# A two-layer streaming encoder on eight cores: weight loads on ScalarE's DMA queue, paired x transfers in flight together, a fourth x slot, the small first group of layer 2 batched, the first sums on VectorE

## What is computed

```python
xn = rms_norm(x, lp['norm_mix'])
proj = xn @ lp['w_in']                      # q | k | v | pool_in | two gates
q = rms_norm(q, ...); k = rms_norm(k, ...)
a = swa_prompt(q, k, v, lp['sinks'])        # each 64-frame chunk reads itself and two before it
pl = pool_mixer(p_ext, pos, w_pool, pool_scale)   # trailing means over 2/4/8/16, minus the token
mix = (g[:, :, 0] * (a @ lp['w_br_attn']) + g[:, :, 1] * (pl @ lp['w_br_pool'])) @ lp['w_out']
x = x + mix
...
h = xn2 @ w_up                              # 1024 -> 2 * 2816
hc = conv_b + sum(conv_w[j] * h_ext[:, j:j + T] for j in range(3))
y = (gelu(gate) * val) @ w_down
x = x + y
```

## Time and profile before

| | |
|---|---|
| runs (us) | 3847.88, 4010.42, 4087.85; median 4010.42 |
| the profiled execution | 3838.31 us, span 3836.7 us on its slowest core |
| spans of the eight cores | 3823.3 to 3836.7 us |
| mean granted TensorE clock | 0.947 to 0.953 of full speed |
| busy in the span | PE 87%, DVE 56%, ACT 40%, POOL 31% |
| chain that ended last, by engine | PE 62%, DMA 17%, DVE 6%, POOL 5%, ACT 4%, issue 4%, SP's queue 1% |

### The profile page before, as it was taken

How to read it: one execution, slowest core, us unless ns; L and a number is a source line. 1 busy time by engine, 2 the same in 40 slices (tenths; PEclk the granted TensorE clock), 3 DMA queues, 4 the chain that set the end, 5 groups by cost and what they waited for, 6 DMA issues and landing times.

```text
span 3836.7 us, 54933 instructions; the slowest of 8 cores (3823.3 to 3836.7 us)
## 1 busy us (share of the span) xinstructions
PE 3345.6 (87%) x17810; PEld 1621.7 (42%) x17810; DVE 2135.0 (56%) x3383; ACT 1545.1 (40%) x2432; POOL 1186.7 (31%) x1084
## 2 busy tenths in 40 slices
PE   1579999996599999999975879999966999999999
PEld 0344444442244444444432434444423455555554
DVE  1345455542376776666643444555426766666666
ACT  1244444431234555444433434433314444444444
POOL 1234443321123333322234333333213222333322
PEclk9789999998799999999987989999988999999999
DMA  6326666446623333333353223233252222222221
GB/s 128 69 74 132 127 130 128 122 109 165 185 79 103 92 85 90 95 98 101 106 170 92 50 82 97 88 94 104 76 192 91 81 73 80 80 79 79 79 64 40
DMA packets 186666, 384.37 MB, mean 100 GB/s; under 512 B 32880, under 2 KB 112400, under 8 KB 178384
## 3 DMA queue, kind: packets, MB, share of 16 engines
q1 hardware_dynamic: 181088, 324.00, 28.0%
q0 software_dynamic: 5296, 56.86, 9.6%
HBM read 368.09 MB, written 115.41 MB: 126 GB/s over the span
## 4 chain that ended last, share of the span: by engine, by line
PE 62%; DMA 17%; DVE 6%; POOL 5%; ACT 4%; issue 4%; SPq 1%; DVEq 0%; ACTq 0%; POOLq 0%
PE psb L413 61%; DMA xsl_67<-xT 3%; POOL win_114 L419 1%; DMA xsl_67<-xm 1%; POOL win_115 L419 1%; DMA xsl_66<-xT 1%; DMA xst__146<-xT 1%; DMA xsl_67<-x 1%; POOL PT_121 L419 1%; DMA xst__147<-xT 1%; DMA xsl_66<-x 1%; DMA xsl_66<-xm 1%; DMA xsl_68<-x 1%; ACT P_0_118 L416 1%; DVE xn_71 L422 1%
## 5 line engine op out<-in xcount | busy, mean ns | idle before, releaser
L419 POOL TENSOR_TENSOR actT<-ug_94,uv_97 128x480 bf16<-128x480 f32 (+3 forms) x126 | 148.7, 1180 | 1057.1 <-ACT ug_94 L416 939.6
L416 ACT ACTIVATE ug_94<-psb,pv 128x480 f32<-128x480 f32 (+3 forms) x144 | 106.4, 739 | 698.2 <-PE psb L413 520.5
L422 DVE SCALAR_TENSOR_TENSOR ug_94<-psb,pv,ug_94 128x480 f32<-128x480 f32 (+3 forms) x288 | 202.7, 704 | 137.5 <-ACT hso L416 73.5
L422 DVE SCALAR_TENSOR_TENSOR uv_97<-psb,pv,uv_97 128x480 f32<-128x480 f32 (+3 forms) x288 | 202.3, 702 | 17.2 <-issue 0.6
L422 DVE SCALAR_TENSOR_TENSOR ug_96<-psb,pv,ug_96 128x480 f32<-128x480 f32 (+3 forms) x252 | 177.6, 705 | 52.4 <-ACT ug_96 L416 27.9
L422 DVE SCALAR_TENSOR_TENSOR ug_95<-psb,pv,ug_95 128x480 f32<-128x480 f32 (+3 forms) x252 | 177.4, 704 | 22.8 <-ACT ug_95 L416 6.7
L419 POOL TENSOR_TENSOR actT<-ug_95,uv_98 128x480 bf16<-128x480 f32 (+3 forms) x126 | 148.7, 1180 | 128.9 <-ACT ug_95 L416 116.4
L422 DVE SCALAR_TENSOR_TENSOR uv_99<-psb,pv,uv_99 128x480 f32<-128x480 f32 (+3 forms) x252 | 177.0, 702 | 14.7 <-DVE uv_99 L422 0.9
L422 DVE SCALAR_TENSOR_TENSOR uv_98<-psb,pv,uv_98 128x480 f32<-128x480 f32 (+3 forms) x252 | 177.3, 704 | 14.0 <-DVE uv_98 L422 0.5
L419 POOL TENSOR_TENSOR actT<-ug_96,uv_99 128x480 bf16<-128x480 f32 (+3 forms) x108 | 127.4, 1179 | 159.3 <-ACT ug_96 L416 120.8
L413 PE MATMUL psb<-xn_71,w_up_83 128*128 128x482 bf16 (+3 forms) x576 | 122.4, 373 | 55.3 <-DVE xsl_68 L422 55.3
(11 more groups left out here) (317 smaller groups left out, 7352.0 us busy)
## 6 DMA issues: line engine op xcount, KB each, us to landing
wb<-wun POOLq DMA_DIRECT2D x42, 1024.0 KB, 9.9
xsl_68<-x SPq DMA_DIRECT2D x35, 512.0 KB, 4.1
xsl_68<-xT SPq DMA_DIRECT2D x31, 512.0 KB, 5.1
xsl_66<-x SPq DMA_DIRECT2D x31, 512.0 KB, 4.9
xsl_67<-x SPq DMA_DIRECT2D x30, 512.0 KB, 5.0
xsl_66<-xT SPq DMA_DIRECT2D x29, 512.0 KB, 5.9
xsl_67<-xT SPq DMA_DIRECT2D x28, 512.0 KB, 5.3
xm<-xsl_67 SPq DMA_DIRECT2D x27, 512.0 KB, 3.3
```

The costliest lines, as they stand in the source:

```text
L416: S.op("act", lambda e: e.activation(out=out, in_=in_, func=func, **kw), reads=reads, writes=writes)
L419: S.op(eng, lambda e: e.tensor_tensor(out=out, in0=a, in1=b, op=op), reads=reads, writes=writes)
L422: S.op("dve", lambda e: e.scalar_tensor_tensor(out=out, in0=a, scalar=s, in1=b, op0=op0, op1=op1), reads=reads, writes=writes)
```

## The change

Weight loads from `wb` are issued by ACT in place of SP, at the same places of the text. A DMA can name the earlier part of its own pair (`chain`) and then doesn't wait for it; x loads, x stores and the first loads use this, and `load_first` is cut into two halves. There are four x slots, so all four pairs of a load or residual can be issued at once. `srt` and `sq` now lie on `tg`, and the tables of attention, the caches and the pool weights lie in the mixer phase and are loaded anew for layer 2 (`tables`). The halo of a pool row has its own resource, and there are three `pinb` buffers. Until layer 1's first two groups are projected, the window adds and the attention product that POOL did are on DVE (`ast["eng"]`). Layer 2's group 0 is normed into a tile `xg0` in the middle of the last `ffn_up`, group 1's sums lie there as well, and group 0 is projected by a new `stage_B_small`, which makes the four pool rows together and the four q rows together; its attention steps move from group 1's `stage_B` to group 2's. Casts move from the last mixer group to the FFN.

```diff
-NXS = 3
+NXS = 4
+FW = 480
...
                 stream_last[op.stream] = op
+                c = op.chain
+                while c is not None:
+                    deps.pop(c, None)
+                    c = c.chain
...
-                dma(wt[n][:, 0:sz], wb[i, :, 0:sz], [f"wb{i}"], wres(n), st)
+                dma(wt[n][:, 0:sz], wb[i, :, 0:sz], [f"wb{i}"], wres(n), st, eng="act")
...
+            c = None
             for (a, b, t) in segs:
-                dma(xs[i][:, :, a:b], src[2 * pair:2 * pair + 2, :, t:t + b - a].rearrange("k p t -> p k t"),
-                    src_res(pair, t, b - a), [f"xs{i}"], f"xs{i}")
+                c = dma(xs[i][:, :, a:b], src[2 * pair:2 * pair + 2, :, t:t + b - a].rearrange("k p t -> p k t"),
+                        src_res(pair, t, b - a), [f"xs{i}"], f"xs{i}", chain=c)
...
-                r = j % 2
+                r = pst["n"] % 3
+                en = ast["eng"]
                 if G.own:
-                    copy("pool", pinb[r][:, 0:16], phist[:, j, :], [f"ph{j}"], [f"pinb{r}"])
-                    act(pinb[r][:, 16:528], psb[:, bk, 0:512], ACTF.Copy, pr(bk), [f"pinb{r}"])
+                    act(pinb[r][:, 16:528], psb[:, bk, 0:512], ACTF.Copy, pr(bk), [pb])
+                    copy(en, pinb[r][:, 0:16], phist[:, j, :], [f"ph{j}"], [ph])
...
-                tt("pool", dst[:, lo:16 + n], cur[:, lo:16 + n], cur[:, lo - d:16 + n - d], ALU.add, [cr], [dr])
+                tt(ast["eng"], dst[:, lo:16 + n], cur[:, lo:16 + n], cur[:, lo - d:16 + n - d], ALU.add, rd, [dr])
...
-            rload(0); rload(1)
+            rload(0); rload(1); rload(2); rload(3)
...
+        def stage_B_small(l, G):
+            qk_job(l, G, wkv, "w_kv", 0, 0, OFF_GK, [(0, N, kg0[:, 0:N], "kg0"), (G.samp, N, kn32s[:, :], "kn32s")])
...
+            copy("pool", pS[:, :, 18:34], sph[:, :, :], ["sph"], pn)
...
+            for i in range(4):
+                d, lo = 1 << i, (2 << i) - 1
+                tt("pool", dst[:, i:4, lo:W], cur[:, i:4, lo:W], cur[:, i:4, lo - d:W - d], ALU.add, cr, [dr])
...
-                stage_B(1, gs[0])
-                copy("dve", xnS[:, :, :], xn0[:, :, gs[0].C0:gs[0].N], ["xn0"], ["xnS"])
+                tables(1)
+                stage_B_small(1, gs[0])
                 job = mix_norm(1, gs[2])
...
-                stage_B(1, gs[1], merged(att_steps(1, gs[0]), js))
+                stage_B(1, gs[1], js)
+                job.loads()
                 job.root()
                 job.scales()
-                stage_B(1, gs[2], merged(att_steps(1, gs[1]), [[lambda g=g: fold_pool(1, g)] for g in range(4)]))
+                stage_B(1, gs[2], merged(att_steps(1, gs[0]) + att_steps(1, gs[1]), [[lambda g=g: fold_pool(1, g)] for g in range(4)]))
...
-                    if m in (1, 3, 5) and i > 0:
+                    if m in (1, 3, 5) and i > 0 and nxt is not None:
                         cast_next()
...
-                    job = mix_norm(1, mg[1][0])
+                    first, job = mix_norm(1, mg[1][0]), mix_norm(1, mg[1][1])
```

More of the change, by code:

```diff
@@ L399, in build_nc, with rows, over @@
         hpo = su("f", "hpo", [128, NCH, 2], F32)
+        def rows(name, n, size):
+            return [(f"{name}{j}", j * size, (j + 1) * size) for j in range(n)]
+        def over(name, base, delta, shape, dt, phase, res):
+            off = offs[base][1] + delta
+            t = nc.alloc_sbuf_tensor_at(name, list(shape), dt, offset=off)
+            for (r, lo, hi) in res:
+                S.region(r, off + lo, off + hi, phase)
+            return t
+        xn1 = su("m", "xn1", [128, KT, 512], BF16)
@@ new lines, in build_nc @@
+        srt = [over(f"srt{i}", f"tg0{i}", 0, [128, 512], F32, "b", [(f"srt{i}", 0, 2048)]) for i in range(2)]
+        sq = [over(f"sq{i}", f"tg1{i}", 0, [128, 512], BF16, "b", [(f"sq{i}", 0, 1024)]) for i in range(2)]
+        expAB = [su("m", f"exp{i}", [128, 8, 128], F32) for i in range(2)]
+        wpt = [su("m", f"wpt{l}", [128, 512], BF16) for l in range(2)]
+        kcache = su("m", "kcache", [128, 128], BF16)
+        Vcache = su("m", "Vcache", [128, 2, 66], BF16)
+        sph = su("m", "sph", [128, 4, 16], F32)
@@ L743, in stage_B, with v_tile @@
                 filler()
+        def v_tile(X, xr, c, n, dst, rn, o):
+            bk = PB.get()
+            wkv = wv("kv", 8)
+            for k in range(KT):
+                mm(psb[0:n, bk, 0:128], X[:, k, c:c + n], wkv[:, k, 128:256], k == 0, k == KT - 1, ["w_kv", xr], pr(bk))
+            src = psb[0:n, bk, 0:128]
+            copy("dve", dst, src.rearrange("p (g d) -> p g d", g=2), pr(bk), [rn])
+            if o is not None:
+                copy("dve", o32[0:n, :], src, pr(bk), ["o32"])
+                dma(o, o32[0:n, :], ["o32"], [], "misc_out", True)
+            PB.put(bk)
@@ L1059, in build_nc, with tables, pool_map @@
         nj1 = mix_norm(0, mg[0][1], keep=(xst1, "xst1_"))
[L1060 to L1061 removed]
+        wraw = [(srt[0][:, :], "srt0"), (P32[0][:, 0:512], "P32_0")]
+        def tables(l):
+            dma(sph[:], sph_d[l], [], ["sph"], "c5")
+            dma(expAB[0][:], expA_d, [], ["exp0"], "c2")
+            dma(expAB[1][:], expB_d, [], ["exp1"], "c3")
+            dma(wraw[l][0], wpt_d[l], [], [wraw[l][1]], "c8")
+            dma(kcache[:], ckT_d[l], [], ["kcache"], "c6", eng="pool")
+            S.op("pool", lambda e: e.memset(Vcache[:], 1.0), writes=["Vcache"])
+            dma(Vcache[:, :, 0:64], cv_d[l], [], ["Vcache"], "c7", eng="pool")
+            S.op("pool", lambda e: e.memset(Vsam[:, :, 64:66], 1.0), writes=["Vsam"])
+            v_ones()
+            S.op("pool", lambda e: e.tensor_copy(out=Vg0[:, :, :, 64:66].rearrange("p t g e -> p (t g) e"),
+                                                 in_=hvt[:, 0:1].unsqueeze(1).to_broadcast([128, 6, 2])),
+                 reads=["hvt"], writes=[f"Vg0_{t}" for t in range(3)])
+        def pool_map(l):
+            for g in range(4):
+                S.op("dve", lambda e, l=l, g=g: e.tensor_scalar(out=wpt[l][:, g * 128:(g + 1) * 128], in0=wraw[l][0][:, g * 128:(g + 1) * 128],
+                                                                scalar1=pvc(l, OFF_PS + g, 1), scalar2=None, op0=ALU.mult),
+                     reads=[wraw[l][1], "pv"], writes=[f"wpt{l}"])
+        ast["eng"] = "dve"
+        nj0.loads()
         dma(pv[:], pvec, [], ["pv"], "c0")
         dma(hvt[:], hv_d, [], ["hvt"], "c1")
[L1064 to L1065 removed]
         for n, dst, src in (("bones", bones, bones_d), ("ones", ones, ones_d)):
@@ L1150, in build_nc @@
                 if nxt is None:
-                    load_w(l, "up0"); load_w(l, "up1")
+                    load_w(l, "up0", "up1")
                 if job is not None:
-                    for p in range(3):
-                        job.load(p)
+                    job.loads()
                 for m in range(KT):
@@ L1186, in build_nc @@
                 if nxt is None:
-                    for n in ("up8", "up9", "up10", "dn0", "dn1", "dn2", "dn3", "dn4", "dn5"):
-                        load_w(l, n)
+                    load_w(l, "up8", "up9", "up10", "dn0", "dn1", "dn2", "dn3", "dn4", "dn5")
                 if i + 2 < len(gs):
@@ L1193, in build_nc @@
                 S.epoch += 1
+                end = g.last and l == 0
+                first = None
                 if i + 1 < NFG:
@@ L1225, in before @@
                         job.root()
-                        for p in range(3):
-                            job.scale(p)
-                        job.load(3)
-                        job.scale(3)
-                    if two is not None:
-                        two.stats()
-                def hook():
-                    two.root()
-                    two.scales()
-                ffn_down(l, g, before, hook if two is not None else None)
+                        job.scales()
+                ffn_down(l, g, before)
         assert not castq
```

338 lines of the change are left out of this document (172 added, 166 removed).

## The result

The changed kernel is slower: the ratio to the kernel before is 1.0345, with an interval of 1.0272 to 1.0417. Its profiled execution took 3977.96 us (span 3976.4); the forecast was 3673, from 3605 to 3765.

The account below looks back on a forecast made before the run. PE was taken to bound the FFNs, with gains only in the mixers' idle time and the seams. 30 + 7 + 25 + 56 + 34 + 13 = 165 us off 3838 gave 3673 us, range 3605 to 3765.

Parts of the forecast that it names:

- The step that failed: FFN of both layers: PE is busy throughout, no edit takes work off it, so its 1723 us stay.
- The start: Before group 0's stage_E: 18 us from POOL's wait plus 12 from x parts, 30 us gained, bounds 10 and 43.
- The 18.06 us: Start: PE's last long wait, for a pinb buffer of POOL's, claimed to go with windows and product on DVE.
- Rival 3: Start: pairs and weights land as before, DVE takes over POOL's lateness; 0 in place of 30, 3703 us, chance 0.13.
- Layer 1, output of group 0: Residual's third pair no longer waits for a slot and a load's second part; 7 us, between 0 and twice that.
- Mixer to FFN: Weight loads in ACT's list: layer 1 gains 56 us (17 stall, 39 upward phase), layer 2 gains 13.
- The waits on up10 and dn5: FFN's first group: first gate tile and first product wait over bytes shared with mixer tiles; claimed to remain.
- Mixers: Steady part, both layers: 25 of 87 us idle gained by third pinb, halo resource and fourth slot; bounds 0 and 45.
- Layer 2's entry: Entry into layer 2: nhl wait 20, group 0's projections 7, stage_F 7, moved attention 0; sum 34, from 5 to 52.
- Rival 1: Mixer to FFN: DMA bandwidth, not SP's list, sets landings; only the 17 remains there, 3725 us, chance 0.17.
- Rival 2: ACT's list after stage_E: ACT held by its loads at 16.18 us a landing, slower, 3869 us, chance 0.04.
- The slower side: Whole kernel: more than 2% slower than before, through landings of 19 us or more, chance 0.03.

Follow-up runs that it names:

- run 1: Changed kernel with the tile width FW back at 512 in place of 480; ratio 0.9651 to the kernel before, 3715.12 us.
- Runs 1 to 5: Changed kernel at width 512 (3715.12 us); kernel before, ug/uv 480 (4008.38); changed kernel with: ug/uv 512 (3705.44), staging overlap left out (3877.91), non-chaining bookkeeping (3467.35).
- run 10: Changed kernel at 512 columns, parts of one load, store or weight unit waiting for each other again; 3749.15 us, ratio 0.9766.
- Run 11: Changed kernel at 512 columns, load of out1 moved behind group 0's stage_B; 3663.43 us, ratio 0.9560.
- run 7: Changed kernel at 512 columns with the weight loads on SP's queue in place of ACT's; 3701.32 us, ratio 0.9638.
- run 6: Kernel before with bookkeeping that no longer notes a write as a write to overlapped tiles; 3655.86 us, ratio 0.9504.

## Why the prediction was wrong

The parts by PE's timeline, from the first matmul of one stage to the first of the next (us):

| part | before | after | gained | forecast | gained at 512 (run 1) |
|---|---|---|---|---|---|
| start to `stage_E` of group 0 | 175.9 | 165.2 | 10.7 | 30 | 8.2 |
| to group 2's projection, layer 1 | 55.5 | 56.2 | −0.7 | 7 | 1.3 |
| mixer, layer 1, without the stall | 673.2 | 652.3 | 20.9 | 25, both layers | 37.9 |
| stall at the end of `stage_E` | 17.1 | 0 | 17.1 | 17 | 17.1 |
| `stage_F` to first `ffn_down` | 170.3 | 153.6 | 16.7 | 39 | 25.1 |
| FFN of layer 1, to its last `ffn_down` | 865.5 | 992.7 | −127.2 | 0 | −17.4 |
| to `stage_E` of group 0, layer 2 | 183.9 | 162.6 | 21.3 | 27 | 21.6 |
| to group 2's projection, layer 2 | 92.7 | 84.9 | 7.8 | 7 | 8.2 |
| mixer, layer 2 | 585.3 | 564.5 | 20.8 | with layer 1 | 34.4 |
| `stage_F` to first `ffn_down` | 151.3 | 151.3 | 0 | 13 | 8.8 |
| FFN of layer 2 and end | 866.0 | 993.1 | −127.1 | 0 | −22.1 |
| sum | 3836.7 | 3976.4 | −139.7 | 165 | 123.1 |

**The step that failed** is the first: "No edit here takes work off PE, so those 1723 us stay." A full PE can't get faster by such edits, but it can get slower, and nothing in my text asked what the new tile width does to the waits there. The 254 us of the two FFN rows turn a gain of 115 into a loss of 140. (That this is also the total of the `ug` waits is chance: those stand all over the span, and part of the loss in the FFN is clock.) Runs 1 to 5 show the cause from both sides: the width alone makes the kernel before 168 us slower and its removal the changed one 267 us faster, and without the chaining the same width costs nothing. Of the 254, some 159 hang on the mixer tiles and the rest on the staging tile. I had used the rule of the bookkeeping for the weight loads and for `ug0` and up10, and did not ask it of `ug` against `uv`.

**The start** was mis-sized by the same omission. The 18.06 us did go. The parts, for which I had counted 12 ahead of the first matmuls, gave 4.8 there; the 23 that run 10 loses at `stage_E` are mostly the landing of out1, which I had not counted. DVE's write of the normed x took the place of the 18. Rival 3 had DVE taking over POOL's lateness, but by `wpt` or by a weight that is needed; it was out1 by way of up10, 30.6 us. Run 11 takes it away and wins more than the 30 of the forecast.

**Layer 1, output of group 0.** The term of 7 gave −0.7. Before the matmuls on `w_kv` at the same place PE still waits 4.60 us for a residual, for 7.38 before:

```profile
221.43 3.57 PE L420 MATMUL psb<-xn_60,w_kv 128*128 128x512 bf16 x8 [4.60 <-DVE xsl_54 L429]
```

The wait, for which I had counted on all of the 7, is 2.8 shorter, and the stretch before it is 3.5 longer.

**Mixer to FFN.** The stall of 17 went, but not by the queue. In the kernel before it is the fourth x pair, which has to wait until the first slot is free again: POOL waits for it, ACT's square for POOL, the gate behind the square in ACT's list, and PE for the gate.

```profile
911.20 0.10 POOL L470 MEMSET xsl_66<- 128x4 f32 x1 [12.72 <-DMA xsl_66<-xm]
911.40 1.01 ACT L416 ACTIVATE xsl_66<-xsl_66 128x964 f32<-128x964 f32 x1 [13.79 <-POOL xsl_66 L470]
913.12 6.56 PE L413 MATMUL psb<-xn_71,w_eg_78 128*128 128x512 bf16 x16 [10.61 <-ACT tg_129 L416]
```

Of the 17 us 10.61 are this wait. The stall stays away with the loads on SP (run 7) and with the parts in a row (run 10), and it stays, 16 us, in run 6, which has three slots and no false waits. What is left is the fourth slot, and casts and loads that moved with it; three slots in the changed kernel were not run. The list on ACT was through 66 us after `stage_E`, forecast 58: four units landed in 7 to 13 us beside the x loads, which is 17 us over the 5.83 and 4.91 of the forecast, in place of the 10 that I had added for x. At 512 the phase gained 25 of 39 and 9 of 13; and the 39 was itself too large by 8, since I had taken the end of the phase from a window's bound, 1100, while the first `ffn_down` starts at 1092. But the reason that I gave, the queue, is refuted by run 7, and of the parts only 3 and 6 us come by run 10. What remains, the four slots and the order of the loads around them, was not tried apart; that is open. The waits on up10 and dn5, of which I wrote that they remain, were worth more: in run 6 the kernel before takes 134 and 109 us for 170 and 151.

**Mixers:** 42 us, forecast 25; at 512 columns 72, the other 30 being lost to the narrow tiles. The waits on the x slots went as said (16.5 us in 300 to 860 before, no row of them in 300 to 815 after), those on `sq` hardly (12.7, now 9.5); where the rest came from is open. **Layer 2's entry:** 29 in all, forecast 34; the wait of 20.60 went, group 0's projection took 10 us (2062.5 to 2072.6) for 20.3, and groups 1 and 2 together, with group 0's attention moved from one to the other, took 6 more. Here the mechanisms were right. Outside the FFN the forecast of 165 stands against 115 at 480 columns and 163 at 512. The second agreement is luck in part: the start (8 of 30) and the change of layer 1 fall short, and the mixers (72 of 25) make up for them.

Rival 1 was right that the queue gives nothing; its time, 3725, is near the run at 512, but for another reason, since the change to the FFN did become shorter. Rival 2's price of 16.18 a landing was not met. The slower side, to which I gave 0.03, came by a mechanism that I had not listed.

## What to carry to other kernels

Where a scheduler notes a write to one tile as a write to all that share its bytes, moving a tile, or resizing it by 128 bytes as here, is an edit of the program's waits: list, before and after, which tiles now share a third, also in stages that the change does not touch. A saturated engine is no cover for such waits; its share of 100% says that nothing can be won, not that nothing can be lost. And make the bookkeeping exact before tuning queues: here that alone was worth 5% to the kernel before and 13% to the changed one (3978 to 3467).
